# First feed-forward net on seven of eight block products, with a down-projection pass of its own

## What is computed

```
x = x + gate1 * mixer_l(modulate(rmsnorm(x, norm1_g), shift1, scale1))
z = modulate(rmsnorm(x, norm2_g), shift2, scale2)
g, v = split(dwconv(z @ w_up, conv_w, conv_b, 1), 2)      # 1024 -> 2 x 2816, three taps along the tokens
x = x + gate2 * ((silu(g) * v) @ w_down)                  # 2816 -> 1024
```

## Time and profile before

| | us |
|---|---|
| median of 3 runs | 2883.98 (2881.82 to 2887.42) |
| profiled execution | 2880.96 |
| its span | 2879.2 |
| TensorE (PE) busy | 2831.8 (98%), 15789 matmuls |
| VectorE (DVE) busy | 1696.1 (59%) |
| ScalarE (ACT) busy | 1137.8 (40%) |
| GpSimd (POOL) busy | 619.4 (22%) |
| granted TensorE clock, mean | 0.996 |

### The profile page before, as it was taken

How to read it: one execution, slowest core, us unless ns; L and a number is a source line. 1 busy time by engine, 2 the same in 40 slices (tenths; PEclk the granted TensorE clock), 3 DMA queues, 4 the chain that set the end, 5 groups by cost and what they waited for, 6 DMA issues and landing times. The chain is left out here.

```text
span 2879.2 us, 39269 instructions
## 1 busy us (share of the span) xinstructions
PE 2831.8 (98%) x15789; PEld 2371.7 (82%) x15789; DVE 1696.1 (59%) x2364; ACT 1137.8 (40%) x1500; POOL 619.4 (22%) x483
## 2 busy tenths in 40 slices
PE   8999999999999999999999999999999999999999
PEld 6888887878888888888887888888787788887888
DVE  7677666276766656665656045545638888885111
ACT  6676874141122121112224244444525444444331
POOL 3322230200000000000014344433424000005653
PEclk9999999999999999999999999999999999999999
DMA  9544434112122222222103443333433222227442
GB/s 341 148 116 113 119 86 169 55 52 66 55 63 66 74 81 66 81 74 74 52 30 98 143 122 93 85 92 82 123 126 103 81 88 85 76 69 261 156 139 72
DMA packets 300084, 293.31 MB, mean 102 GB/s; under 512 B 43763, under 2 KB 260178, under 8 KB 297856
## 3 DMA queue, kind: packets, MB, share of 16 engines
q1 hardware_dynamic: 284576, 236.45, 27.0%
q0 software_dynamic: 15296, 54.35, 6.1%
q10 hardware_dynamic: 32, 0.01, 0.0%
HBM read 241.29 MB, written 46.47 MB: 100 GB/s over the span
## 5 line engine op out<-in xcount | busy, mean ns | idle before, releaser
L758 PE MATMUL ps<-zH,wH 128*128 128x512 f32 (+1 forms) x1392 | 494.4, 355 | 2.0 <-DVEq L2552 2.0
L758 PE MATMUL ps<-zL,wH 128*128 128x512 f32 (+1 forms) x1392 | 492.9, 354 | 0.0
L758 PE MATMUL ps<-zH,wL 128*128 128x512 f32 (+1 forms) x1392 | 492.5, 354 | 0.0
L758 PEld LDWEIGHTS ps<-zH,wH 128*128 128x128 f32 x1392 | 263.2, 189 | 47.1 <-issue 7.8
L758 PEld LDWEIGHTS ps<-zL,wH 128*128 128x128 f32 x1392 | 263.3, 189 | 36.4
L758 PEld LDWEIGHTS ps<-zH,wL 128*128 128x128 f32 x1392 | 263.1, 189 | 36.6
L4157 POOL TENSOR_TENSOR slotL<-slotS,slotH 128x512 fp32r<-128x512 f32 x88 | 125.0, 1429 | 451.4 <-ACT slotH L4087 451.4
L2571 DVE SCALAR_TENSOR_TENSOR res<-ps,mod,res 128x1024 f32<-128x1024 f32 (+1 forms) x160 | 134.1, 880 | 102.1 <-PE ps L758 94.7
L2212 POOL DMA_DIRECT2D modw<-in_mod_w_dram x24 | 21.3, 886 | 764.7 <-DVE acc L2662 764.7
L2972 POOL TENSOR_SCALAR S<-S,rowstat 128x608 f32<-128x608 f32 (+1 forms) x63 | 136.0, 2158 | 199.3 <-DVE rowstat L3267 199.3
L3179 ACT ACTIVATE S<-S,rowstat 128x640 f32<-128x640 f32 (+1 forms) x128 | 103.5, 809 | 144.2 <-DVE rowstat L3262 144.2
(11 more groups left out here) (452 smaller groups left out, 6822.2 us busy)
## 6 DMA issues: line engine op xcount, KB each, us to landing
modw<-in_mod_w_dram POOLq DMA_DIRECT2D x40, 1024.0 KB, 5.8
wraw<-in_ffn_w_up_dram SPq DMA_DIRECT2D x77, 512.0 KB, 4.0
slotS<-in_ffn_w_down_dram SPq DMA_DIRECT2D x88, 256.0 KB, 2.8
wraw<-in_na_w_in_dram SPq DMA_DIRECT2D x32, 512.0 KB, 4.1
bias<-scratch_bias SPq DMA_DIRECT2D x512, 32.0 KB, 1.8
wraw<-in_ffn_w_down_dram SPq DMA_DIRECT2D x22, 512.0 KB, 3.4
scratch_h<-V SPq DMA_DIRECT2D x22, 512.0 KB, 2.6
scratch_xT<-res SPq DMA_DIRECT2D x16, 512.0 KB, 5.5
```

The costliest lines, as they stand in the source:

```text
L758: last = nc.tensor.matmul(ps[:, slot * SLOT + c:slot * SLOT + c + n], w(k), r(k)[:, c:c + n], start=(k == 0 and i == 0), stop=(k == K - 1 ...
```

## The change

`ffn` is gone. Phase `front` now ends with `up_first` and `down_first`; the attention is a phase of its own, `middle`, whose first loads and weight splits (`attention_start`) are made at the end of `front`.

```diff
-    up = ffn(nc, m, 0, TOK, norm2, norm1, att)
+    norm2 = SummedPieces(nc, m, "n01", 0, 1, TOK, None)
+    down = down_first(nc, m, m.norm1, m.start)
+    up = up_first(nc, m, norm2, down)
...
-    in_turn(nc, [rg, pr, up, att])
+    in_turn(nc, [rg, pr, up, down])
+
+
+def middle(nc, m):
+
+    in_turn(nc, [attention(nc, m, m.norm1, m.start)])
...
-    m.hD = nc.dram_tensor("scratch_h", [KF, P, SEQ], F32).ap()
+    m.hD = nc.dram_tensor("scratch_h", [KF, P, TOK], F32).ap()
```

**up_first** keeps blocks 0 and 1 as four plain units (g0, v0, g1, v1; `first_done` counts 8 pieces). Blocks i = 2 to 21 are tiles of seven products on halves of 640 tokens, in two rounds p of 320 columns; a round is 7 x 4 x 3 matmuls:

```diff
+    HALFT, COLS = TOK // 2, TOK // 4
+    MADE = (A11, A22, S1, S2, A12, S3, S4)
+    USED = (A11, S2, A12, S3, S1, S4, A22)
...
+        def product_of(i, p, x):
+            pe.wait_ge(w_low, SPLITS.index((i, x)) + 1)
+            bank_free(i, p, x)
...
+            for k in range(4):
...
+                for n, (wt, z) in enumerate(((wH, zH), (wH, zL), (wL, zH))):
...
+        for i, p in ROUNDS:
+            for x in USED:
+                product_of(i, p, x)
```

In `bank_free`, product A12 of a round waits for `snapped` (ACT has copied A11's bank), S3 for `formed` "s16", A22 for "u3". The weights of a tile lie in nine pages of 256 KB; `FirstSlots` gives a product of the next tile the page that was freed first, so that the sum S3 of tile i+1 is written where S3 of tile i lies, and waits for its product of round 1 (`slot_free`). On DVE a tile is:

```diff
+            if i > HEAD:
+                c21(i - 1, 1)
+                taps_g(i - 1)
+                s16(i, 0)
+                taps_v(i - 1)
+                u3(i, 0)
+                gated(i - 1)
...
+            sum_of(i + 1, S1)
+            sum_of(i + 1, S2)
+            s16(i, 1)
+            sum_of(i + 1, S3)
+            low(i + 1, A11)
+            low(i + 1, A22)
+            u3(i, 1)
+            sum_of(i + 1, S4)
+            low(i + 1, S1)
+            low(i + 1, S2)
+            low(i + 1, A12)
+            x12(i, 1)
+            c22(i, 1)
+            low(i + 1, S3)
+            c12(i, 1)
+            low(i + 1, S4)
```

```diff
+            elif PAGES + 5 <= n < PAGES + 5 + KD:
+                k = n - PAGES - 5
+                sp.dma_start(m.res[:, k, :], m.xT[k]).then_inc(res_in, 16)
...
+    STEP_AT = [MOD_FROM + 3 * q for q in range(MOD_STEPS)]
...
+        def add(n, y):
...
+            chunk_done(dve, n)
+            dve.wait_ge(res_in, 16 * KD)
...
+        def turn(n):
+            pe.wait_ge(mod_row, 2 * n + 2)
...
+            if split3(n)[2] == NX - 1:
+                add(n, 0)
+                add(n, 1)
...
+            for b, last in ((1, LAST_PASS), (2, TWO + LAST_PASS)):
+                for x in range(NX):
+                    if n == last + (x if b == 1 else released(x)) + 1:
+                        low(dve, b, x)
+            for chain in SUM_AT.get(n, []):
+                columns(chain)
```

More of the change, by code:

```diff
@@ L1632, in rg_out @@
     w = m.t["rg_w_out"][0]
-    y_in = [sem(f"p0_y_in{k}") for k in range(KD)]
+    y_in = m.landed
     y_high, y_low = sem("p0_y_high"), sem("p0_y_low")
@@ L1718, in sync @@
             load_w(sp, mt)
+            for k in {5: (0, 1), 6: (2,), 7: (3,)}[mt]:
+                nxt.spill_row(sp, k)
+        nxt.early_sync(sp)
     def w_high_of(act, mt):
@@ L2730, in fcol, with attention_start, place, early_sync @@
     return m.vec[:, ds(col + at, 1)]
-def attention(nc, m, norm):
+def attention_start(nc, m):
+    sem = m.kept_sem
+    part = Bag()
+    part.raw_in = raw_in = [sem("na_raw_in0"), sem("na_raw_in1")]
+    part.w_high, part.w_ready, part.spilled = w_high, w_ready, spilled = sem("na_w_high"), sem("na_w_ready"), sem("na_spilled")
+    w_in = m.t["na_w_in"][0].rearrange("(k p) n -> p k n", p=P)
+    def place(i):
+        return (i + FIRST_PLACE[0]) % 3
+    def early_sync(sp):
+        for n, at in enumerate((D, 0)):
+            part.prev.page_free(sp, place(n))
+            sp.dma_start(m.wraw[:, place(n), :].rearrange("p (k n) -> p k n", k=KD), w_in[:, :, at:at + P]).then_inc(raw_in[n], 16)
+    def spill(sp, k):
+        sp.wait_ge(part.prev.item_added, 2 * KD)
+        sp.dma_start(m.xT[k][:, 0:SEQ], m.res[:, k, 0:SEQ]).then_inc(spilled, 16)
+    def early_scalar(act):
+        act.wait_ge(raw_in[0], 16)
+        part.prev.page_free(act, 3 + place(0))
+        part.prev.page_free(act, 6 + place(0))
+        nc.scalar.activation(m.wH[:, place(0), :], m.wraw[:, place(0), :], ACT.Copy).then_inc(w_high, 1)
+    def early_vector(dve):
+        dve.wait_ge(w_high, 1)
+        nc.vector.tensor_tensor(m.wL[:, place(0), :], m.wraw[:, place(0), :], m.wH[:, place(0), :].bitcast(F32), ALU.subtract).then_inc(w_ready, 1)
+    part.spill, part.early_sync, part.early_scalar, part.early_vector = spill, early_sync, early_scalar, early_vector
+    return part
+def attention(nc, m, norm, start):
     t, sem, ps = m.t, m.sem, m.ps
@@ L2908, in sync @@
             store_v(e)
-        sp.wait_ge(part.prev.mod_row, part.prev.sums)
         sp.wait_ge(v_out, 16 * 16)
@@ L2972, in scale @@
             nc.gpsimd.tensor_scalar(x, x, m.rowstat[:, g % 2, 5:6], None, ALU.mult).then_inc(scaled[1], 1)
-        w_low(gp, 1)
+        norm.add(gp, 3 * (KD - 1), *norm.pieces[2], last_sq(KD - 2), 3 * KD - 1)
+        gp.wait_ge(w_ready, 2)
         w_low(gp, 2)
@@ new lines, with __init__ @@
+class FirstSlots:
+    PAGES = (2, 0, 1, 3, 6, 4, 7, 5, 8)
+    MADE = (A11, A22, S1, S2, A12, S3, S4)
+    USED = (A11, S2, A12, S3, S1, S4, A22)
+    def __init__(self):
+        free = [(page, None) for page in self.PAGES]
+        self.page, self.freed_by = {}, {}
+        for i in range(HEAD, KF):
+            for x in self.MADE:
+                self.page[i, x], self.freed_by[i, x] = free.pop(0)
+            for x in self.USED:
+                free.append((self.page[i, x], (i, x)))
+        self.left = dict(free)
```

1562 lines of the change are left out of this document (944 added, 618 removed).

## The result

| | before | after |
|---|---|---|
| median | 2882.9 us | 3005.98 us (3004.12 to 3007.48) |
| ratio | | 1.0424, 95% interval 1.0406 to 1.0442 |
| profiled execution, its span | 2880.96, 2879.2 | 3005.64, 3003.9 |

The account below looks back on a forecast made before the run. PE, busy 98% issuing matmuls, was taken as the bound. Savings and added waits summed to +9.9 us on the profiled 2880.96, giving 2891, plus 3.0 for the median: 2894 us; 8-in-10 range 2852 to 2916.

Parts of the forecast that it names:

- Fewer products: Up_first's 20 tiles: 168 matmuls of 320 columns, 24.64 us a tile instead of 27.5; -57.6 us.
- Tile boundary: Up_first: PE waits 1.3 us for ACT's snap and 0.45 for s16, 19 times; +32 us.
- Rival B: Tile boundary closed: c12 comes at 12.3, so the snap is ready for A12; 2864 us, chance 0.12.
- rival D: Waits at each tile boundary drop the clock to 1.2 GHz, some 1.2 us more a tile; 2917 us, chance 0.10.
- Head: Start of up_first: PE at unit v1 waits 8.4 us for v1's low on DVE, plus clock and later lows; +11.7 us.
- Entry and barrier: Attention's entry: loads made early but a barrier ahead, about 30.7 us instead of 33.5; -2.8 us.
- Last block: End of the down pass: 256-column chunks of 1.44 us against z and lows on DVE; +1 us (0 to 5).
- hand-over: Into the down pass: low of gated rows 8 and 9 lands late, behind c21 and taps; +3.4 us.
- Turns in the down pass: PE's turns wait for DVE's chains, delayed by the residual reload and block 1's lows; +26 us (8 to 40).
- The clock: Down pass: half clock after waits, 1.6 us at the turn behind chunk 14 and 3 at later turns.
- Rival E: Down pass limited by DMA, waits of 10 to 20 us more; 2908 us, chance 0.14.
- Rival A: Turns hardly wait if the last residual row lands by chunk 13 and lows fit between chains; 2870 us, chance 0.15.

Follow-up runs that it names:

- e4: The change with DVE's order at the up_first tile boundary altered so that c12 comes sooner, most lows behind it; 2969.93 us, 1.03.
- e5: The change with v1's low ahead of sum S3 on DVE, and ACT's split of the first down weights behind the last tile's c11; 2991.61 us, 1.0382.
- e1: The change with POOL clearing the down weights' low parts from chunk 7 on instead of forming them, so writing without reading SBUF; 2953.74 us, 1.0242.
- e2: The change with DVE, not POOL, forming the low parts of the down weights from chunk 7 on; 2967.79 us, 1.0293.
- e9: e7 with POOL keeping lows of chunks 7 to 11, gated-row lows moved in DVE's order, turns five chunks behind their chains; 2870.94 us, 0.9957.
- e7: The change with e4, e5 and e2's edits, first residual additions later, modulation steps spaced wider, turns three chunks behind chains; 2882.05 us, 0.9997.
- e8: The change with each modulation chain's seven additions in down_first done on 8 of 256 columns; 2964.08 us, 1.0282.
- e10: The change with e1 and e8 together and the first quad's residual additions moved to chunk 14; 2926.91 us, 1.0151.

## Why the prediction was wrong

**Fewer products, -57.6: right.** Matmuls of 320 columns start 0.147 apart as the line through the earlier trace rows had it, and in e4, where nothing waits, PE is busy without a gap.

**Tile boundary, +32: right in mechanism and place, near in size.** 19 waits of 1.3 us for the snap and 19 of 0.35 for s16, 31.4 us; forecast 1.3 and 0.45. e4 took them away and won 36. Rival B ("c12" in time) fell, and rival D with it: the granted clock stays at 1.00 through these waits. The tiles still took 21 us more than forecast: 6.5 are ACT's wait in the last tile, which had no term, 2.3 the passage to the down pass, 1.3 a wait for A22's moving side, which the prediction had counted with the head. A tile lasts 26.76 us (snap waits at 866.55 and 893.31 by the matmul's start), 0.47 more than 24.64 and the waits, some 9 us over 19. The starts around the waits account for it. The trace counts an idle time from the end of the matmul before, 0.31 us behind its start, where the next would have started after 0.147: 0.16 more for each of the two waits. And the matmul behind each wait is followed at 0.22 and not at 0.147: 0.08 more for each.

**Head, +11.7: right in the wait, short in the clock.** The wait was 8.3 for 8.4, by the releaser named. The head lost 5 more: 1.6 us were put down for the clock, and the granted clock was 0.89 over the 77 us (597.66 to 674.84). e5 took both this and the unforeseen ACT wait away, for 14.4.

**Entry and barrier, -2.8: near.** 2.9 us for the barrier and 26.2 for the matmuls are 29.1, 4.4 less than the 33.5 of before. The prediction's own terms (25 + 3 + 1.6) add up to 29.6 and not to the 30.7 it wrote.

**Last block, +1, and hand-over, +3.4.** The hand-over's wait was 4.1. In the last block PE waited 6.1 us for POOL's lows (chunks 110 to 118), where DVE's had been feared.

**Turns in the down pass, +26: this is the step that failed.** The mechanism named (turns wait for chains) and two of its places (the reload ahead of step 1's chains, block 1's lows) are in the trace, but the term was worked out with 4.0 us a chain, from a row of a stretch in which POOL did nothing. The sentence "Later DVE has 8.7 us of chains per three chunks of 8.2 and a turn of 0.56, just balanced" is where it goes wrong. Its 8.7 us are two chains of 4.0 and the reduction of a turn, 0.68. With POOL's lows beside them, the two chains alone took 10.8 us (1296.41 to 1307.24) and 13.1 (1332.40 to 1345.46). A term in balance has no reserve, so all of it goes to PE: 73 us of waits for 21. The bound of 40 did not hold it, since it was made from late loads and not from slower operations. PE's waits at the turns, in us, turn by turn:

| turns behind chunk | forecast | the change | e1, POOL not reading |
|---|---|---|---|
| 11 | 0 | 6.8 | 2.1 |
| 14 | 10 | 12.5 | 13.1 |
| 17 to 32, six turns | 0 | 13.6 | 3.3 |
| 37, 43, 49 | 11.4 | 27.4 | 15.5 |
| the five behind 49 | 0 | 12.8 | 0.4 |

With POOL's reads gone the waits lie mostly where the forecast had them, 34.3 us in all for 21.4. So POOL stands for some 39 of the 52 us that the term lacked (32 by e2, where DVE takes the lows over). The rest stays with POOL out of the way: late loads, the order, and a balance that had no reserve even at full speed.

**The clock: mis-sized.** I put 4.6 us of half clock into the down pass. Its length to the barrier less matmuls, turns, sums and the waits ahead of the barrier (436.9 - 302.7 - 9 - 3.6 - 89.5) leaves 32 us. Of these 24 can be seen in the starts: 128 matmuls of 512 columns are followed, without a wait, at over 0.24 us instead of 0.227, 94 of them at 0.40 to 0.44. The eight matmuls at half rate behind one wait became fifteen waits of up to 12.5 us, close to each other, with a mean granted clock of 0.81 in the worst 50 us.

**Rival E** (DMA in the down pass) had the place and not the main cause: DMA share is 0.56 there, and e9's pass runs at 0.71 and is 87 us shorter. Rival A's condition did not come: the last row of the residual was there at 1283.13, as chunk 14 ended, and not at chunk 13.

## What to carry to other kernels

A duration read from a trace holds for what ran beside it. Before moving DVE work to a stretch where POOL forms low parts, or the other way about, take for each POOL operation that reads SBUF up to its full 1.3 us off DVE's time. Here it was 0.76 us in the mean by DVE's busy time in e1 (78 us less for 103 lows) and 0.89 by e2. If the DVE operation it would save is shorter (0.68 to 0.73 here), leave it on DVE. And a term that comes out as just balanced is a risk of full size, not a zero: here 11 to 13 us of DVE work for 8.7 of PE, eight times.

On an engine that works in order, ask of each wait what stands behind it that somebody else needs. The snap, v1's low, c11 and the first additions were waits of that kind. What e4 and e5 won came from order alone, and what e9 won over e7 from order and from five lows given back to POOL.

## What the runs showed that was not expected

- The standstill has nothing to do with the size of DVE's operation: 227 ns became up to 4735 ns with 8 columns (e8). Where POOL only writes, it stays at 225 to 229 (e10).
- Operations with one tensor operand in SBUF are hit too: the first operation of a chain (L3785, TENSOR_SCALAR) has a mean of 537 to 575 ns in the change and 0.34 us where POOL rests. Unlike the additions it is held by POOL's writes too: in e10 the one at 1284.43 took 1176 ns while POOL did nothing but clear (1283.98 to 1285.45). The means of e10, 403 and 543 ns, do not show this by themselves, since single long rows make them and one of these (2371 ns) has POOL's additions beside it. The Trainium skill's page "SBUF — State Buffer" has that as well (Who interferes with whom: tensor_scalar can enter a mode that takes both ports).
- PE keeps its 2.4 GHz level through 38 waits of 0.35 and 1.3 us, two for each 26.8 us (granted clock 1.00 from 690 to 1190 us).
- POOL's own issue of the 1 MB loads cost the additions nothing that can be seen. In e1 such an issue lies over 52 additions that keep their 485 ns, and in e2, where only those issues and POOL's additions for the norm are left, the mean of L3787 is 494 ns.
